# A fourth pass's input stage put ahead of the first block, and the final norm put behind the next block's first section

## The reference

```python
h = rmsnorm(x, norm_mix_g)
u = h @ w_in                       # 2,832 columns: inputs and gates of four groups
mix = concat(lru(u), ssd(u), gdn(u), s5(u))     # recurrent along the tokens
x = x + mix @ w_out
x = x + cross_attend(rmsnorm(x, norm_cross_g), mem_k, mem_v, w_cq, w_co)
x = x + swiglu(rmsnorm(x, norm_ffn_g), w_gate, w_up, w_down)    # hidden 2816
y = rmsnorm(x, norm_final_g)
```

## The kernel before

| | end of A0 | A1 | fv | A2 | w, att of B0 | ffn0 | w1, att1 | ffn1 | A3 | w2, att2 | ffn2 | A4 | w3, att3 | ffn3 |
|---|---|---|---|---|---|---|---|---|---|---|---|---|---|---|
| steps | 22 | 34 | 4 | 27 | 24 | 64 | 14 | 63 | 11 | 11 | 48 | 8 | 13 | 54 |

## Time and profile before

### The profile page before, as it was taken

The page is one execution under the profiler, slowest core; times in us unless marked ns, Lnnn a source line. Parts: engine busy times, 40 slices in busy tenths (PEclk is TensorE's granted clock), DMA queues, the critical chain, the costliest instruction groups (busy, mean ns, idle before and its releaser), DMA issues.

```text
span 3811.7 us, 61402 instructions
## 1 busy us (share of the span) xinstructions
PE 3481.6 (91%) x23786; PEld 3101.4 (81%) x23786; DVE 2145.2 (56%) x4395; ACT 1289.8 (34%) x2325; POOL 90.8 (2%) x288
## 2 busy tenths in 40 slices
PE   6778888888899888999999889999988999989998
PEld 6766767775898877788888787888888899989998
DVE  6657657373776755755667345445573655544223
ACT  5453344341544434332333233222233331223001
POOL 2200000000000000000000000000000000000000
PEclk9998899989999999999999999999999999999999
DMA  5674544658555575555666834555567555576776
GB/s 203 217 263 164 192 152 172 227 186 251 188 183 186 170 276 177 193 197 204 226 222 221 288 144 161 177 176 180 183 209 289 189 203 194 204 262 224 252 250 213
DMA packets 329074, 787.83 MB, mean 207 GB/s; under 512 B 29904, under 2 KB 148560, under 8 KB 328400
## 3 DMA queue, kind: packets, MB, share of 16 engines
q1 hardware_dynamic: 301968, 748.90, 56.3%
q10 hardware_dynamic: 26816, 35.01, 2.5%
HBM read 609.22 MB, written 174.57 MB: 206 GB/s over the span
## 4 chain that ended last, share of the span: by engine, by line
issue 52%; PE 37%; DVE 4%; ACT 2%; POOLq 2%; DVEq 1%; DMA 1%; ACTq 1%; POOL 0%; SPq 0%
PE banks L483 11%; PE banks L485 11%; PE banks L484 11%; PE banks L1712 1%; ACT whi_sb L963 1%; PE banks L1682 0%; DMA wlo_sb<-kept_dram 0%; DVEq L1277 0%; DVE uc_sb L1313 0%; DVE hl_sb L1238 0%; DVE rstd_sb L1381 0%; POOLq L2220 0%; POOLq L2218 0%; PE banks L1692 0%; DVE m_p_sb L2287 0%
## 5 line engine op out<-in xcount | busy, mean ns | idle before, releaser
L483 PE MATMUL banks<-hh_sb,whi_sb 128*128 128x384 f32 (+1 forms) x2800 | 1054.1, 376 | 83.8 <-DVE hl_sb L1238 26.5
L484 PE MATMUL banks<-hh_sb,wlo_sb 128*128 128x384 f32 (+1 forms) x2800 | 1023.5, 366 | 0.0
L485 PE MATMUL banks<-hl_sb,whi_sb 128*128 128x384 f32 (+1 forms) x2800 | 1023.0, 365 | 0.0
L483 PEld LDWEIGHTS banks<-hh_sb,whi_sb 128*128 128x128 f32 x2800 | 541.1, 193 | 152.0 <-issue 41.1
L485 PEld LDWEIGHTS banks<-hl_sb,whi_sb 128*128 128x128 f32 x2800 | 538.9, 192 | 50.3
L484 PEld LDWEIGHTS banks<-hh_sb,wlo_sb 128*128 128x128 f32 x2800 | 540.9, 193 | 46.3 <-issue 1.3
L483 PE MATMUL banks<-g_hi_sb,whi_sb 128*128 128x384 f32 (+2 forms) x1264 | 458.7, 363 | 28.2 <-DVE x_sb L1427 15.5
L485 PE MATMUL banks<-g_lo_sb,whi_sb 128*128 128x384 f32 (+2 forms) x1264 | 447.0, 354 | 0.0
L484 PE MATMUL banks<-g_hi_sb,wlo_sb 128*128 128x384 f32 (+2 forms) x1264 | 446.8, 353 | 0.0
L1427 DVE TENSOR_TENSOR x_sb<-x_sb,banks 128x384 f32<-128x384 f32 (+3 forms) x336 | 193.8, 584 | 285.6 <-PE banks L485 265.5
L1219 DVE TENSOR_TENSOR wlo_sb<-raw_sb,whi_sb 128x1024 fp32r<-128x1024 f32 x203 | 248.2, 1226 | 143.6 <-ACT whi_sb L963 139.3
(11 more groups left out here) (448 smaller groups left out, 4717.4 us busy)
## 6 DMA issues: line engine op xcount, KB each, us to landing
whi_sb<-kept_dram SPq DMA_DIRECT2D x392, 512.0 KB, 3.6
wlo_sb<-kept_dram SPq DMA_DIRECT2D x392, 512.0 KB, 4.8
raw_sb<-w SPq DMA_DIRECT2D x176, 512.0 KB, 4.6
kept_dram<-whi_sb SPq DMA_DIRECT2D x112, 512.0 KB, 5.1
kept_dram<-wlo_sb SPq DMA_DIRECT2D x112, 512.0 KB, 5.9
uc_dram<-uc_sb ACTq DMA_DIRECT2D x54, 192.0 KB, 3.2
uc_dram<-uc_sb ACTq DMA_DIRECT2D x36, 256.0 KB, 2.0
plain_sb<-w SPq DMA_DIRECT2D x32, 256.0 KB, 4.7
```

What stands on the lines that cost most here:

```text
L483: eng.matmul(out, xh, yh, start=first, stop=False)
L484: eng.matmul(out, xl, yh, start=False, stop=False)
L485: return eng.matmul(out, xh, yl, start=False, stop=last)
```

## The change

- **Order.** A3 now follows A2, ahead of B0; only A4 is laid behind a block, B1 (`LATE_AFTER = 1`), in the place that A3 had there. So: A0, A1, A2, A3, B0, B1 + A4, B2, B3, B4. Window 0 ends with A3's `u` sections; window 2 is B1 and A4; window 3 is B2 alone.
- **A3's and other preps.** A3's eight preps go through `g_free` in one go at z2.1; no mixer step may stand behind that section. Pass 4's ones take A3's way of before.
- **Where blocks adjoin** (0 to 1, 2 to 3, 3 to 4): the next pass's `w.0` stands ahead of `st` and `final`. Its residual input is loaded to `g_free` (`sp_residual`) once the last `d` has read it, and w.0's to w.7's sums are read from there and written to x (`dve_add`); w.0's sum is done behind the last scaling. The stores to `y_t` there are issued from ACT's queue (`store_final`), no longer from SyncE's.
- **`ldb` has four tiles** (`LDS` 3 to 4). To make room: `yo` lies in `p2` (with one more wait, on `xs5`), the table `eye64` is gone (one DVE operation on 128 partitions is two on 64), `c5` and `etotb` lie in other tiles, `raw12` has three places for two, and some semaphores are merged.

Steps per stage, from the same rule:

| | end of A0 | A1 | fv | A2 | A3 | w, att of B0 | ffn0 | w1, att1 | ffn1 | A4 | w2, att2 | ffn2 | w3, att3 | ffn3 |
|---|---|---|---|---|---|---|---|---|---|---|---|---|---|---|
| steps | 20 | 26 | 3 | 23 | 15 | 24 | 64 | 15 | 62 | 11 | 13 | 54 | 14 | 53 |

```diff
+LATE_AFTER = 1
-RAWS, SPLITS, LDS, KVS = 3, 4, 3, 7
+RAWS, SPLITS, LDS, KVS = 3, 4, 4, 7
...
-    def stage_b(p, hy):
+    def stage_b(p, hy, end):
...
+        if end:
+
+            out[1].squares = out[0].squares + out[1].squares
+            out[0].squares = []
+            out[1:1] = end
...
-    for p, part in ((1, kv[:-4]), (2, kv[-4:])):
+    early = 1
+    for p, part in ((1, kv[:-4]), (2, kv[-4:]), (3, [])):
         h, n = new_h("A", p), new_norm("A", p)
-        spread(part[-8:] if p == 1 else part, preps("A", p, h, n))
+        items = preps("A", p, h, n)
+        if part:
+            spread(part[-8:], items)
+        else:
+
+            for x in items:
+                x.early = early
+            early += 1
+            spread(secs[-1:], items)
         secs += part + stage_a(p, h, n)
...
-        if 0 < p < NP - 2:
-            h, n = new_h("A", p + 2), new_norm("A", p + 2)
+        if p == LATE_AFTER:
+            h, n = new_h("A", NP - 1), new_norm("A", NP - 1)
...
+        def dve_add(eng, s):
+
+            n, out = cols(s.p), x[:, s.a, 0:cols(s.p)]
+            dve_preps(eng, before_adds(s))
+            bank = bank_in(eng, s.f)
+            if s.p in RESIDUAL:
+                if s.a == 0:
+                    eng.wait_ge(y_loaded, 64 * RESIDUAL[s.p] + 64)
+                if s.a % 2 == 0:
+                    eng.wait_ge(out_stored[s.a // 2], 32 * s.p)
+                before = g_free[:, s.a // 4, s.a % 4, 0:n]
...
+            eng.tensor_tensor(out, before, bank[:, 0:n], ALU.add).then_inc(x_done, 1)
+            eng.drain().then_inc(free[s.f % 3], 1)
...
+                if s.a == KD - 2 and s.p + 1 in RESIDUAL:
+                    dve_add(eng, next(o for o in SECS if o.kind == "w" and o.p == s.p + 1))
...
+        def store_final(eng, s):
+
+            t0, n = PASSES[s.p][0] * P, cols(s.p)
+            for k in (s.a, s.a + 1):
+                eng.wait_ge(out_ready, KD * s.p + k + 1)
+                eng.dma_start(t["y_t"][:, k, t0:t0 + n], x[:, k, 0:n]).then_inc(out_stored[k // 2], 16)
...
+        def sp_residual(eng, i):
+
+            eng.wait_ge(full, SECS[i].f)
+            p = SECS[i].p
+            t0, n = PASSES[p][0] * P, cols(p)
+            for q in range(KD // 2):
+                eng.dma_start(g_free[:, q // 2, q % 2 * 2:q % 2 * 2 + 2, 0:n],
+                              t["x_t"][:, 2 * q:2 * q + 2, t0:t0 + n]).then_inc(y_loaded, 16)
```

More of the change, by code:

```diff
@@ L272, in schedule @@
         first = len(secs)
-        b = stage_b(p, hy)
+        b = stage_b(p, hy, end)
         secs += b
-        last = [secs[-4 + i] for i in range(4)]
-        if 0 < p < NP - 2:
-            h, n = new_h("A", p + 2), new_norm("A", p + 2)
+        last = [s for s in b if s.kind == "d"][-4:]
+        if p == LATE_AFTER:
+            h, n = new_h("A", NP - 1), new_norm("A", NP - 1)
             ups = [s for s in b if s.kind == "up"]
-            spread(ups[8:8 + KD], preps("Q", p + 2, -1, n))
-            spread(last, preps("A", p + 2, h))
-            a = stage_a(p + 2, h, n)
+            spread(ups[8:8 + KD], preps("Q", NP - 1, -1, n))
+            spread(last, preps("A", NP - 1, h))
+            a = stage_a(NP - 1, h, n)
         else:
@@ L299, in schedule @@
                 s.squares = [(fin, 2 * s.b), (fin, 2 * s.b + 1)]
-            a = [st] + end
+            end = [st] + end
         secs += a
+        if a:
+            end = []
         if p + 1 < NP:
-            windows.append((p + 1, first, len(secs) - (2 if secs[-1].kind == "z" else 11)))
+            windows.append((p + 1, first, len(secs) - (2 if secs[-1].kind == "z" else 6)))
+    secs += end
     w = f = ld = sq = n = q = kvn = ev = cv = g = gev = 0
@@ L359, in schedule @@
         s.after = w
-    return secs, hs, ns, uses, w_fill, fills_of_h, windows
-SECS, HS, NS, USES, W_FILL, H_FILLS, WINDOWS = schedule()
+    return secs, hs, ns, uses, w_fill, fills_of_h, windows, residual
+SECS, HS, NS, USES, W_FILL, H_FILLS, WINDOWS, RESIDUAL = schedule()
 N_W = len(USES)
@@ L422, in may_follow @@
     s = SECS[i]
-    return not (s.kind == "w" and s.a == KD - 1 or i + 1 < len(SECS) and SECS[i + 1].kind in ("st", "pt"))
+    return not (s.kind == "w" and s.a == KD - 1 or s.kind == "z" and bool(s.preps) and s.preps[0].kind == "A" or i + 1 < len(SECS) and SECS[i + 1].kind in ("st", "pt"))
 CHUNK_SECTIONS, SAMPLE_SECTIONS, SCALAR_SECTIONS, N_SETUP = 21, 25, 4, 16
@@ L1188, in act_section @@
                 eng.drain().then_inc(free[s.f % 3], 1)
+            elif s.kind == "final" and s.p + 1 in RESIDUAL:
+                store_final(eng, s)
             elif s.kind == "vo" and s.p == 0 and s.a == 0:
@@ L1370, in dve_second @@
                 dve_norm_tail(eng, SECS[i])
+        def dve_add(eng, s):
[8 more added lines that the diff above has]
+                before = g_free[:, s.a // 4, s.a % 4, 0:n]
+            else:
+                if s.a == 0:
+                    eng.wait_ge(x_loaded, 64 * sum(p not in RESIDUAL for p in range(s.p + 1)))
+                before = out
+            eng.tensor_tensor(out, before, bank[:, 0:n], ALU.add).then_inc(x_done, 1)
+            eng.drain().then_inc(free[s.f % 3], 1)
         def dve_section(eng, i):
@@ L1611, in sp_section @@
                     sp_cache(eng, k)
-            elif s.kind == "final":
-                for k in (s.a, s.a + 1):
-                    eng.wait_ge(out_ready, KD * s.p + k + 1)
-                    eng.dma_start(t["y_t"][:, k, t0:t0 + n], x[:, k, 0:n]).then_inc(out_stored[k // 2], 16)
+            elif s.kind == "final" and s.p + 1 not in RESIDUAL:
+                store_final(eng, s)
         per_chunk = dict(
@@ L2073, in act_chunk @@
             k.need("ssdy")
+            k.need("xs5", 1)
             if k.sample:
@@ L2595, in dve_chunk @@
             if k.sample:
+                eng.drain()
                 dve_select(eng, k, 0)
```

99 lines of the change are left out of this document (53 added, 46 removed).

## The result

The changed kernel takes 3785.48 us in the median (3784.15 to 3786.98, 4 runs), the kernel before 3809.01 us (3805.47 to 3811.61, 4 runs) beside it: a ratio of 0.9931, 95% interval 0.9919 to 0.9943, or 26 us less. 50 were forecast. The profiled execution has a span of 3783.7 us where it had 3811.7.

The account below looks back on a forecast made before the run. PE's instruction stream was taken as the bound. The terms -26 - 3 - 3.6 - 2 - 8 - 4 - 3 summed to -50 us: 3763.5 for the profiled execution, 3761 us against the median, with a range from 3722 to 3797.

Parts of the forecast that it names:

- Window 0: Input stages A1 to A3: 64 steps spread wider, fewer two-step sections, -26 us; A0 loses two steps, -3.
- the content rival: Window 0: a step costs its content wherever it stands, part 1 gives 0 to -5, result 3786 us; chance 0.16.
- prices 2.4 and 2.75 at `z` and `fv`: Window 0: estimated us per mixer step at z and fv sections, between the lone step and the double one.
- A3 without a final norm: Input stages A3 and A4: 24.2 us for A4 plus 11 for A3, together 35, against 48.4 before.
- the slower rival: A3's sections wait for kept weights; at 4 us in all 20, +30 us, 3841; chance 0.05.
- The new meeting of 2 and 3: Where blocks 2 and 3 adjoin: PE waits 8.1 us with all banks full, 9.6 with the clock.
- 0 meets 1: Where blocks 0 and 1 adjoin: w1.0 evicted at 1395 instead of 1406, w1.3 starts 8 us earlier, -8.
- 3 meets 4: Where blocks 3 and 4 adjoin: eviction at 3408.4 instead of 3415.8, partly used by PE already, -4 us.
- The step at nothing for ACT's issues: Meetings: ACT's eight store issues hold ACT only until DVE has scaled; what is queued behind waits anyway; no cost.
- the meetings are bound by transfers: Rival: the residual lands no earlier, part 4 gives nothing, the new meeting costs 18.8 instead of 9.6; 3782 us; chance 0.12.
- The fourth tile: Fourth `ldb` tile: 3 of ACT's 4.7 us waiting for x tiles ahead of A2 go, -3 (none to 5).
- At nothing: One more DVE operation in each of 17 chunks and the `xs5` waits lie under PE; up to 1 us in A1.

Follow-up runs that it names:

- the run with the narrow window: The changed kernel with window 0 over input stages A1 and A2 alone, A3 in its new place without steps: 0.9986 of the kernel before.
- the run with fewer steps: The changed kernel with three mixer steps, at sections 4 to 6, instead of five in the output sections of passes 1 and 3: 0.9918 of the kernel before.

## Why the prediction came out as it did

The sign was right and the time lies within the range, but the sum was twice too large: 50 us for 26. That 3785 us is also where the two rivals of the range stood (3786 and 3782) is chance, since neither's mechanism is what was found. Step by step:

1. *Window 0* (-26 and -3 for A0): right in kind, 21 by the run with the narrow window, and the content rival, which gave 0 to 5, falls with it. But A0's two steps alone are 9.7 of this (257.0 for 247.3), so the window proper gave about 12 where 26 were set. The prices were off: by a window for each section, 27 `u` of A1 and A2 with one step have 7.8 us in the mean (the first 8.0, the last 7.7), 2.2 over the floor and not 1.75; 7 with two have 9.7 (14.1 and 9.1), 4.1 over it and not 5.6. With 27 and 7 that nearly cancels. The mis-sized term is that of the "prices 2.4 and 2.75 at `z` and `fv`", which were estimates: the four z sections took 80.7 us for a floor of 44.3, 36 us for eight steps, 4.5 each. In the kernel before they took 62.2 (467.1 to 503.5 and 702.6 to 728.4) with six steps, so they grew by 18.5 us where the sum had 5. Those of the changed kernel:

```profile
434.50:458.70 24.20, 21.07 (x147) 20.69 (x145) 12.24 (x47) 6.87 (x10) 1.19 (x3) 0.85 0.56 192
458.70:480.20 21.50, 17.20 (x137) 16.48 (x136) 12.72 (x44) 5.53 (x12) 0.00 (x0) 0.90 0.50 179
646.80:668.60 21.80, 16.90 (x160) 16.19 (x158) 10.88 (x25) 9.91 (x20) 0.00 (x0) 0.90 0.67 243
668.60:681.80 13.20, 12.84 (x98) 12.66 (x97) 2.63 (x6) 5.13 (x9) 0.00 (x0) 0.90 0.09 32
```

2. *A3 without a final norm* (11 us naked): 104.3 - 91.4 = 12.9 in the narrow run. Its 15 steps cost 2.0 each, not 1.75. The late weights of the slower rival didn't come: A3 took 134.1 us, and PE waited 3.1 us for kept weights in it, in two places. A4 kept its surroundings, 26 us beyond floor and steps where 24.2 were set.

3. *The new meeting of 2 and 3*: PE's idle time once the banks are full was 8.4 us against 8.1. That agreement is partly luck: without the wait for the store it is 6.0 to 6.2. And the term ended there, and the step that the plan put ahead of the preps cost another 4.1 us of waiting. The window has 72.3 us; with 49.8 for floors and 7.5 for five steps, 15 are left where 9.6 were set.

4. *0 meets 1* (-8) failed, and *3 meets 4* (-4) gave -2.4. The failed step is "then waits 11.85 us, until 1405.7, for the residual": the chain behind it was taken over without asking what else the first sum needs. It needs its tile's store to have landed. With this wait gone the forecast chain holds: with the stores on SyncE `w.0` is evicted 33.3 us into the window, and 1395 in the forecast was 34.0 into it. The step at nothing for ACT's issues ("what is queued behind them, w.1's squares and the split of w.3's weights, waits for w.1's sum anyway") counted what ACT's issues hold up, not what SyncE, now free, would send beside them. The rival "the meetings are bound by transfers" was near: the DMA engines were full for 27.6 us and the sum waited for a transfer; but its reason, a residual that lands no earlier, was wrong. The plan's fifth step, which the forecast had not in it, cost some 3 us more of waiting (4.7 with it, 1.5 without) beside its own work.

   Of the rule set against this part (the Trainium skill, DMA: Bandwidth & Descriptors, "Issuing engines are not separate DMA queues") the landings agree: issued by ACT, the stores landed in 9.6 us beside SyncE's transfers, and in 2.4 us ahead of them. The section says that only issue time is saved; that time can be lost as well is what these runs add.

5. *The fourth tile* (-3): about -6, not settled within 0 to 12.

6. *At nothing* failed for the split: "they may cost up to 1 us" is 5 to 6 us for the split, measured twice on the kernel before. The cover that was named, VectorE's spare time in the feed-forward, is not there in input stage 1.

Outside all terms stands a gain of 12 us: attention and feed-forward of pass 3, up to the last group of `d`, fell from 448.2 to 436.0 us, the kernel before first:

```profile
2929.90:3378.10 448.20, 433.88 (x3412) 413.63 (x3411) 251.50 (x566) 132.59 (x273) 0.00 (x0) 0.98 0.55 197
```

```profile
2916.50:3352.50 436.00, 428.15 (x3389) 409.20 (x3390) 248.72 (x563) 123.91 (x260) 0.00 (x0) 0.99 0.58 200
```

The gain goes with the new meetings: with these undone the same stretch takes 448.2 us again. That pass 3's steps begin one section earlier fits this and the run with fewer steps, where pass 3 lost; what in those steps makes it was not tried.

The shortfalls are then 8 (window and A0), 4 (stages), 5 and 12 (meetings) and 5 (split), 34, less 3 for the tile and 12 for pass 3: 19, for a gap of 24. Items from different runs, each good to some 5 us or worse, don't close better than that.

## What to carry to other kernels

When a wait is taken away, list everything that the waiting instruction needs, above all stores that still read what it overwrites, and take the next latest. Before transfers go to a second engine's queue, look at what the first engine holds back while it waits: if that is large and not urgent, the wait was ordering the traffic. When a plan is shifted by one place, look for the step that now stands ahead of work on which PE waits.

## What the runs showed of the hardware

0.41 us more of VectorE's work in each chunk lengthened input stage 1 by 7.3 us, of which 6.0 are PE's own busy time: in two of its windows the granted clock fell from 0.94 to 0.85 and from 0.90 to 0.77, means between its levels of 1.2 and 2.4 GHz. And a single issue on SyncE's queue took 6.80 us in the stretch where the DMA engines were full, the one ahead of it 0.44; in the run with the stores on SyncE, in a stretch as full, the same issue took 0.76 and the longest 3.67, so a full share alone does not set it.
